# First expert block of a mixture-of-experts kernel: one-hot placed ahead of the counts, fewer count operations, table columns turned by two ScalarE loads

## What is computed

```python
logits = (xt @ w_router + b_router)
top_val, top_idx = lax.top_k(logits, TOP_K)          # 4 of 32 experts
gates = jax.nn.softmax(top_val, axis=-1)
counts = jnp.bincount(flat_e, length=N_EXPERTS)
# tokens of one expert are packed into blocks; then for each block:
xb = xt[tok]
gu = xb @ w_gate_up[e] + b_gate_up[e]
act = (up + 1.0) * gate * jax.nn.sigmoid(SWIGLU_ALPHA * gate)
yb = act @ w_down[e] + b_down[e]                     # times the gate, summed per token
```

## Time and profile before

| | us |
|---|---|
| median of 3 runs | 1328.78 (1327.48 to 1328.99) |
| the profiled execution | 1328.35 |
| its span in the trace | 1326.6 |
| TensorE busy | 1255.3 (95%) |
| VectorE busy | 523.0 (39%) |
| ScalarE busy | 194.7 (15%) |
| GpSimd busy | 159.5 (12%) |
| DMA over the span | 455.70 MB, mean 344 GB/s |

### The profile page before, as it was taken

The page is one execution under the profiler, slowest core; times in us unless marked ns, Lnnn a source line. Parts: engine busy times, 40 slices in busy tenths (PEclk is TensorE's granted clock), DMA queues, the critical chain, the costliest instruction groups (busy, mean ns, idle before and its releaser), DMA issues.

```text
span 1326.6 us, 52719 instructions
## 1 busy us (share of the span) xinstructions
PE 1255.3 (95%) x21817; PEld 738.1 (56%) x21817; DVE 523.0 (39%) x1741; ACT 194.7 (15%) x445; POOL 159.5 (12%) x262
## 2 busy tenths in 40 slices
PE   8999999999998999999999999999999999988881
PEld 4545655445565656655655656556656656544451
DVE  6454223346332433433433433333433433422338
ACT  4431123332000000000000000000000000000002
POOL 4100420123101011011010011011011011001000
PEclk9999999999999999999999999999999999999996
DMA  7453131519899999999999999999999999999996
GB/s 227 142 189 126 33 145 53 203 47 365 324 417 418 414 405 417 416 416 411 418 415 418 410 417 416 418 411 417 412 408 417 413 416 415 417 417 418 417 422 259
DMA packets 96886, 455.70 MB, mean 344 GB/s; under 512 B 11057, under 2 KB 23018, under 8 KB 63498
## 3 DMA queue, kind: packets, MB, share of 16 engines
q1 hardware_dynamic: 92784, 445.69, 83.4%
q0 software_dynamic: 3888, 8.40, 1.7%
q10 hardware_dynamic: 106, 0.04, 0.0%
HBM read 432.53 MB, written 23.27 MB: 344 GB/s over the span
## 4 chain that ended last, share of the span: by engine, by line
DMA 51%; PE 46%; DVE 2%; issue 1%; SPq 0%; ACT 0%; ACTq 0%; POOLq 0%; DVEq 0%
DMA ring<-in_w_gate_up_dram 30%; DMA ring<-in_w_down_dram 19%; PE ps L1822 14%; PE ps L1400 11%; PE ps L1853 6%; PE ps L1420 4%; PE ps L1788 2%; PE ps L1461 2%; PE ps L1454 1%; DMA x_rows_dram<-cat,rowi 1%; PE ps L1814 0%; DMA ring<-x_rows_dram 0%; DVE ring L1355 0%; DMA ring<-in_ffn_norm_w_dram 0%; PE ps L1844 0%
## 5 line engine op out<-in xcount | busy, mean ns | idle before, releaser
L1822 PE MATMUL ps<-ring,cat 128*32 128x256 f32 x9856 | 550.8, 381 | 12.5 <-DMA ring<-in_w_gate_up_dram 12.5
L1822 PEld LDWEIGHTS ps<-ring,cat 128*32 128x32 f32 x9856 | 301.2, 110 | 233.5 <-DMA ring<-in_w_gate_up_dram 17.4
L1853 PE MATMUL ps<-ring,cat 128*32 128x256 f32 x4928 | 284.6, 380 | 18.5 <-DMA ring<-in_w_down_dram 18.4
L1853 PEld LDWEIGHTS ps<-ring,cat 128*32 128x32 f32 x4928 | 145.9, 110 | 128.2 <-DMA ring<-in_w_down_dram 21.6
L1400 PE MATMUL ps<-hbuf,ring 128*128 128x512 f32 x320 | 145.8, 601 | 0.4 <-DVE hbuf L871 0.4
L1214 DVE TENSOR_REDUCE wslot<-ps 128x2 f32<-128x6 f32 x77 | 12.6, 163 | 330.7 <-ACT cat L804 329.5
L574 POOL DMA_INDIRECT pair_rows_dram<-cat,rowi x75 | 74.8, 997 | 479.4 <-ACT cat L804 474.3
L799 ACT ACTIVATE cat<-cat 128x128 f32<-128x128 f32 x154 | 47.7, 310 | 523.6 <-DVE cat L1230 523.6
L1788 PE MATMUL ps<-hbuf,cat 128*32 128x256 bf16 x2464 | 106.6, 273 | 1.5 <-DVE cat L1282 1.5
L1230 DVE TENSOR_SCALAR cat<-ps 128x128 f32<-128x128 f32 x154 | 44.9, 291 | 135.8 <-PE ps L1822 135.7
L1400 PEld LDWEIGHTS ps<-hbuf,ring 128*128 128x128 f32 x320 | 58.3, 190 | 66.5 <-issue 64.9
(11 more groups left out here) (330 smaller groups left out, 793.4 us busy)
## 6 DMA issues: line engine op xcount, KB each, us to landing
ring<-in_w_gate_up_dram SPq DMA_DIRECT2D x256, 1024.0 KB, 10.0
ring<-in_w_down_dram SPq DMA_DIRECT2D x128, 1024.0 KB, 10.1
ring<-in_w_in_dram SPq DMA_DIRECT2D x10, 1024.0 KB, 6.4
pair_rows_dram<-cat SPq DMA_DIRECT2D x4, 2048.0 KB, 11.0
ring<-pair_rows_dram SPq DMA_DIRECT2D x4, 2048.0 KB, 21.6
ring<-in_w_out_dram SPq DMA_DIRECT2D x1, 4096.0 KB, 12.7
ring<-in_x_dram SPq DMA_DIRECT2D x4, 512.0 KB, 5.3
x_rows_dram<-ring SPq DMA_DIRECT2D x2, 1024.0 KB, 11.2
```

The costliest lines, as they stand in the source:

```text
L1822: last = mm(ps[SLOTS * q:SLOTS * (q + 1), gu_bank(half), 0:2 * P].rearrange("p (s j i) -> p s j i", s=2, j=4), xgT[:, SLOTS * u:SLOTS * (u ...
L1853: last = mm(ps[SLOTS * q:SLOTS * (q + 1), 1, 0:QD], actT[:, c // 4, SLOTS * (c % 4):SLOTS * (c % 4 + 1)], w[:, i, q * QD:(q + 1) * QD], st ...
```

## The change

- `hot` for block 1 is made on VectorE right behind `rows_T(1)`, ahead of the softmax sums and the counts, instead of between the two halves of block 0's SwiGLU.
- The block counts take four operations up to the minimum for expert 0 (L1255) instead of six: the sum is written to the integer tile directly from PSUM, and the maximum reads the integer tile; two copies are gone.
- `tables_turned` and its two matmuls are gone from TensorE. ScalarE waits for `ebc_ok` 2 after the two sigmoids of block 0 and issues two DMAs, each from 128 partitions of one float32 to 128 neighbouring numbers of `tabf`, which is partition 0 of `cat`. Behind them in its stream stands the copy `ys` of block 0. VectorE waits for both DMAs (`tab_in`) instead of for `tab_ps` and copies from `tabf`.

```diff
@@ in the tiles @@
+        tabf = cat[0:1, 1792:1792 + 2 * P]
@@ ScalarE, activate(g) @@
                     A(sg[:, half], gc[:, half], ACT.Sigmoid, scale=ALPHA).then_inc(sg_ok, 1)
+                if isinstance(g, int):
+                    act.wait_ge(ebc_ok, 2)
+                    for i in range(2):
+                        act.dma_start(tabf[:, i * P:(i + 1) * P], ebc[:, i:i + 1]).then_inc(tab_in, 16)
                 act.wait_ge(w_used, g * NU + NU)
@@ VectorE @@
             rows_T(1)
+            step(V.tensor_tensor(hot[:, :, :, :], slots_at(SLOTS), mine_first, ALU.is_equal), hot_ok, 2)
             dve.wait_ge(texp_ok, 1)
...
             dve.wait_ge(rank_ps, TB + 1)
-            link(V.tensor_scalar(nbf[:, 0, :], ps[:, 4, TB * E:(TB + 1) * E], float(SLOTS - 1), None, ALU.add))
-            link(V.tensor_copy(nbi[:, :], nbf[:, 0, :]))
+            link(V.tensor_scalar(nbi[:, :], ps[:, 4, TB * E:(TB + 1) * E], float(SLOTS - 1), None, ALU.add))
             link(V.tensor_scalar(nbi[:, :], nbi[:, :], SLOTS.bit_length() - 1, None, ALU.arith_shift_right))
-            link(V.tensor_copy(nbf[:, 0, :], nbi[:, :]))
-            link(V.tensor_scalar(nbf[:, 0, :], nbf[:, 0, :], 1.0, None, ALU.max))
+            link(V.tensor_scalar(nbf[:, 0, :], nbi[:, :], 1.0, None, ALU.max))
...
             step(V.tensor_copy(gie[:, :, :], gip[:, :, 0, :]), sel_step, 2)
-            step(V.tensor_tensor(hot[:, :, :, :], slots_at(SLOTS), mine_first, ALU.is_equal), hot_ok, 2)
             swiglu_half(0, 1)
...
-            dve.wait_ge(tab_ps, 2)
-            link(V.tensor_copy(tab[0:1, E + 1:USED], ps[0:1, 5, 0:2 * P]))
+            dve.wait_ge(tab_in, 2 * 16)
+            link(V.tensor_copy(tab[0:1, E + 1:USED], tabf))
@@ TensorE @@
-            def tables_turned():
-
-                pe.wait_ge(ebc_ok, 2)
-                for i in range(2):
-                    last = mm(ps[0:1, 5, i * P:(i + 1) * P], ebc[:, i:i + 1], ident, start=True, stop=True)
-                last.then_inc(tab_ps, 1)
...
             down(0, 0)
-            tables_turned()
             numbers(1)
```

More of the change, by code:

```diff
@@ L265, in moe_block @@
             "bias_out", "bias_home", "gi_ok", "less_ok", "h2p_ok", "first_ok")]
-        part_ps, part_ok, zeroed, rest_ps = [sem(n) for n in ("part_ps", "part_ok", "zeroed", "rest_ps")]
+        part_ps, part_ok, zeroed, rest_ps, tab_in = [sem(n) for n in ("part_ps", "part_ok", "zeroed", "rest_ps", "tab_in")]
         def chain(eng, s, start=0):
```

## The result

| | us |
|---|---|
| before, median of 22 executions | 1328.76 (1327.41 to 1330.08) |
| after, median of 22 executions | 1330.36 (1327.95 to 1333.9) |
| ratio | 1.0014, 95% interval 1.0008 to 1.0020 |
| the profiled execution after, its span | 1329.94, 1328.2 |

The kernel became 1.6 us slower by the medians (2.0 by the means), where 1.4 us faster was forecast. It is inside the stated range (to 1330.4) and within 0.2% of no change, but on the other side, and the interval excludes equality.

The account below looks back on a forecast made before the run. DMA and TensorE carry 97% of the chain; TensorE's block 1 start sets the end. Span 1326.6 - 1.4 = 1325.2, with 1.75 around it 1326.95; against the median, 1328.78 - 1.4 = 1327.4 us; range 1324.9 to 1330.4.

Parts of the forecast that it names:

- the wait of 2.2 us before block 1's gather: TensorE, ready at 326.95, was to stand until 329.2 for the one-hot made from the table.
- the landing: ScalarE's second table load, issued at 320.9, was to land at 323.9: 3.0 us taken, 1.5 and 5.04 kept.
- The fall of the clock in block 0: Lower clock behind TensorE's 1.48 us wait, priced on gather and down: 0.82 + 0.77 = 1.6 us.
- gain is 330.6 - 329.2 = 1.4 us: Block 1's gather on TensorE was to start at 329.2 instead of 330.60, the forecast's whole gain.
- rival D: At `tab_in`, the table through DMA bounds; break-even landing 4.4 us, 2.8 with a clock fall; 1329 to 1331; chance 0.12.
- by the same amount: Any shift of the end of block 1's down was to move the kernel's end equally.
- so they can move without moving the end: Clock falls at 404 and 1275 lie beside the chain's DMAs, so moving them was to cost nothing.
- the prediction's own last sentence: Wrong in kind if block 1's gather doesn't wait for the one-hot, or its shift is missing at 339 and the end.
- rival E: Block 1 moves, but a later stage absorbs it; time about 1328.8 us; chance 0.05.

Follow-up runs that it names:

- the first profile: The changed kernel's first profiled execution, with an on-time table: 1329.94 us, span 1328.2.
- the other six profiles with the whole change: Changed kernel twice more; block 1 written out on TensorE (1.0009); that with 18 unread matmuls (1.0010); loads from two queues (0.9999); weight unit 17 issued later (1.0001).
- its form with unit 17 late: Kernel before, with weight unit 17 (1 MB) issued behind the table instead of ahead of it: ratio 1.0003 (0.9994 to 1.0012), mean -0.02 us.
- the loads alone: Kernel before with only ScalarE's two table loads in place of `tables_turned`: ratio 1.0011 (1.0002 to 1.0020), mean +1.1 us.
- filling: Kernel before plus 12 matmuls whose result nobody reads, in TensorE's wait ahead of block 0's gather: ratio 1.0005 (0.9996 to 1.0014), mean +0.07 us.
- the late profiles: Changed kernel's second and third profiles and that of the two queues; block 1 ends 32.02, 32.23 and 31.51 us behind block 0's row transpose start.
- the one-hot alone: Kernel before with only block 1's one-hot moved early on VectorE: ratio 1.0009 (1.0000 to 1.0018), mean +1.3 us.
- the two queues: Changed kernel with one of the two table loads issued by SyncE, the other by ScalarE: ratio 0.9999 (0.9990 to 1.0009), mean +0.4 us.
- with filling matmuls: Kernel before with the shorter counts and 8 unread matmuls ahead of block 0's gather: ratio 0.9996 (0.9987 to 1.0005), mean -0.88 us.

## Why the prediction was wrong

- **The local steps held in the first profile.** The one-hot ahead of the counts, the second operation of the counts held to GpSimd's end (309.21 against 309.18), no wait and no fall at block 0's gather, ScalarE free for `ys`, the wait of 2.2 us before block 1's gather (2.18 found), the end of its down within 0.15 us. Some of this was luck: ScalarE's issues were undersized (0.56 and 0.65 us instead of 0.38 each) and the landing oversized (2.69 instead of 3.0), and the two nearly cancel in that profile. Block 0's first SwiGLU half was forecast 0.1 us earlier than before and came 0.04 later there, and 0.2 later in five of the other six profiles with the whole change.
- **The fall of the clock in block 0, priced at 1.6 us.** This price was read on TensorE's rows alone. Without the fall, the kernel before is next held by VectorE's `ebc_ok` at the table matmuls and ends block 1 only 0.62 us earlier. The forecast's "gain is 330.6 - 329.2 = 1.4 us" is a difference to an execution with the fall, and 1.2 us of it were found; against one without, 0.6 us are left. How many executions have the fall isn't known: the profiles of the kernel before and of its form with unit 17 late have it behind a wait of 1.48 us, that of the loads alone has the same wait (1.47) and full clock. This lowers the gain and doesn't turn its sign; taking the fall away by filling left the mean where it was (+0.07).
- **The step that failed first: the landing, "I take 3.0 us".** It isn't one number (2.4 to 4.5 us were found), and the prediction read the DMA share in the wrong place: it had the second load issued at 320.9 and gave "0.43 busy in 322 to 323". The same view of the kernel before, a little earlier:

```profile
320.00:321.00 1.00, 1.00 (x24) 0.57 (x20) 0.83 (x6) 0.00 (x0) 0.00 (x0) 1.00 0.96 393
321.00:322.00 1.00, 1.00 (x28) 0.52 (x20) 0.86 (x5) 0.00 (x0) 0.00 (x0) 1.00 0.68 270
```

Up to 321 us, the time of the issue by the forecast itself, the weights run at 0.96; the change had moved the issue to there. In the late profiles they kept their rate to 322.0, 1.5 us longer than in the changed kernel's first, and the landing was 4.0 to 4.5 us, past the break-even of rival D (2.8 us with a fall). In two of three profiles of the changed kernel D is what happened, at its place `tab_in`, with block 1 ending 1.7 and 1.9 us late where D reached to 2.2. I gave it 0.12 and priced the fall apart from the landing. The profiles tie them: the fall was there in each of the three with a wait of 2.8 us or longer.
- **The step that failed second: the transfer to the end.** The prediction has the end of the kernel move "by the same amount" as block 1, and puts the other falls of the clock at nothing, "so they can move without moving the end". The fall that stood at 1275 beside a weight DMA before stands at 1288 on TensorE's stretch of the chain in the first profile after, and costs 1.7 us. There block 1 is 1.2 us earlier and span less T0 1.0 us longer (1021.9 against 1020.9); the late fall makes up for the gain and 0.5 us more, and the other 0.5 is within the scatter. The earlier start is still there where the weights take over (340.90 - 306.33 = 34.6 behind T0 against 341.51 - 305.70 = 35.8), and is gone at the end: by the prediction's own last sentence it is wrong in kind. In its terms this is rival E and a bit more: not only absorbed, but overpaid. It had 0.05.
- **What stays open.** Of three profiles of the changed kernel one was on time and two late. At that rate block 1 ends on average at (29.09 + 32.02 + 32.23) / 3 = 31.1 behind T0, 0.8 us above the kernel before; the means are 1.2 to 2.0 above. The other 0.4 to 1.2 us would fit a late fall of 1.3 to 2.9 us in some executions, but three profiles can't give its share, and whether the change makes it more frequent wasn't tested. Also open are the losses of the one-hot alone and of the loads alone (1.3 and 1.1 us) with block 1 no later than before and full clock near 1288, the gain of the two queues, and why the weights' rate drops 1.5 us earlier in some executions than in others.

No version beats both kernels beyond doubt. The shorter counts alone come nearest: 0.9988 (0.9979 to 0.9998) on one chip, 0.9997 (0.9988 to 1.0006) on another, and on a third, with filling matmuls, 0.9996 (0.9987 to 1.0005). They shorten TensorE's wait before block 0's gather from 1.48 to 0.95 us, with full clock behind it, and bring in one of 0.48 us at the table matmuls.

## What to carry over

When a stall or a clock fall is to disappear, rebuild the kernel's schedule without it first, and count the gain from the engine that is late next; here the price read on the stalled engine's own rows was 1.6 us and the gain 0.6. A gain of a microsecond at one place is worth no more than what the later stages leave of it: ask which other falls of the clock can come onto the chain. Before a tiny DMA replaces two matmuls on the way to a wait, look at the DMA share at the moment of its issue in the *new* schedule: beside the weights it landed 1.0 to 2.1 us later here, and the longer wait that it opened had a fall of the clock behind it.

## What the runs showed of the hardware

- Two loads of 128 x 4 bytes inside SBUF landed 2.4 to 3.0 us behind the second issue where the weights' rate had dropped before it, and 4.0 to 4.5 where they still ran at some 410 GB/s (eight profiles). ScalarE took 0.56 us to issue the first and 0.6 to 1.3 the second.
- At block 1's gather, waits of TensorE of 1.9 to 2.2 us were followed by full clock, and waits of 2.8, 3.2 and 3.6 us by the lower level. At block 0's gather a wait of 1.48 us was followed by the lower level in two profiles, and one of 1.47 by full clock in a third. The length of the wait alone doesn't decide it.
- A fall of the clock cost 1.3 to 2.9 us where TensorE carried the chain (near 1288), and 0.6 us of its 1.6 where VectorE was late next (block 0).
- A VectorE operation on 32 numbers per partition was held to the end of a GpSimd operation in flight and took 0.97 us, whichever operation it was: a copy with a cast before, an integer shift after.
- Between `numbers` and the next bias, where TensorE's program loads a register, 0.14 us passed when TensorE hadn't waited at the table matmuls, and 0.40 to 0.69 when it had. Why isn't shown.
